# Dots of gathered expert rows in another instruction form, mask building moved behind the gathers, and two packing copies moved to ScalarE, in a two-block transformer kernel

## The reference

```python
q = (xc @ w_query).reshape(PEER_TOKEN_CHUNK, PEER_HEADS, 2, PEER_HALF)
s1 = jnp.einsum('thd,hnd->thn', q[:, :, 0], sub_keys_1)
s2 = jnp.einsum('thd,hnd->thn', q[:, :, 1], sub_keys_2)
v1, i1 = lax.top_k(s1, PEER_TOPK)
v2, i2 = lax.top_k(s2, PEER_TOPK)
cand = (v1[..., :, None] + v2[..., None, :]).reshape(...)
cand_idx = (i1[..., :, None] * PEER_NKEYS + i2[..., None, :]).reshape(...)
best, pos = lax.top_k(cand, PEER_TOPK)
idx = jnp.take_along_axis(cand_idx, pos, axis=-1)
g = jax.nn.softmax(best, axis=-1)
u = expert_u[idx]
act = jax.nn.gelu(jnp.einsum('td,thkd->thk', xc, u), approximate=False)
w = g * act
return jnp.einsum('thk,thkd->td', w, expert_v[idx])
```

## Time and profile before

| what | value |
|---|---|
| three runs | 1679.87, 1680.56 (median), 1681.11 us |
| the profiled execution, its own time | 1683.74 us |
| its span, first to last instruction | 1682.0 us |
| mean granted TensorE clock | 0.993 |
| busy: PE, DVE, ACT, POOL | 96%, 62%, 53%, 66% of the span |

### The profile page before, as it was taken

One profiled execution on the slowest core, in us unless ns is written; L12 is line 12 of the kernel. 1 busy time (PEld: TensorE's weight loads), 2 busy tenths in 40 slices (PEclk: granted clock), 3 DMA queues, 4 the chain that ended last, 5 costly groups with the idle time before them and its releaser, 6 DMA issues.

```text
span 1682.0 us, 29977 instructions
## 1 busy us (share of the span) xinstructions
PE 1619.4 (96%) x9740; PEld 1438.8 (86%) x9740; DVE 1041.9 (62%) x2176; ACT 895.5 (53%) x1631; POOL 1105.4 (66%) x604
## 2 busy tenths in 40 slices
PE   8989999999998898999999999999999999899998
PEld 7867899999888888999999897978888787788887
DVE  6274378996799987877888657653222367432223
ACT  5565555555444454555555557435545656554554
POOL 4815779999777776331332187448888895588886
PEclk9999999999999999999999999999999999999999
DMA  6633546665555557897888464125555564255553
GB/s 219 181 101 133 179 165 200 208 205 200 188 192 192 180 175 286 322 326 262 307 318 301 140 192 128 38 76 189 191 187 193 172 183 127 96 178 191 191 190 122
DMA packets 92531, 320.72 MB, mean 191 GB/s; under 512 B 10528, under 2 KB 10528, under 8 KB 92192
## 3 DMA queue, kind: packets, MB, share of 16 engines
q1 hardware_dynamic: 82272, 284.00, 50.9%
q0 software_dynamic: 9216, 33.56, 5.4%
q10 hardware_dynamic: 960, 2.13, 0.4%
HBM read 318.04 MB, written 1.05 MB: 190 GB/s over the span
## 4 chain that ended last, share of the span: by engine, by line
PE 84%; DVE 9%; issue 3%; ACT 2%; POOL 2%; DMA 0%; DVEq 0%; SPq 0%; POOLq 0%; ACTq 0%
PE col L980 10%; PE acc L682 7%; PE acc L683 7%; PE acc L684 7%; PE col L1335 7%; PE acc L1022 6%; PE col L984 5%; PE col L1339 4%; PE acc L1026 3%; PE col L1022 3%; PE mb L1022 3%; PE col L1026 2%; PE mb L1026 2%; PE col L719 1%; DVE expert_rows L2917 1%
## 5 line engine op out<-in xcount | busy, mean ns | idle before, releaser
L2146 POOL TENSOR_TENSOR w_lo<-w_raw,w_hi 128x1024 fp32r<-128x1024 f32 (+2 forms) x394 | 932.9, 2384 | 276.2 <-ACT w_hi L1551 248.9
L1551 ACT ACTIVATE w_hi<-w_raw 128x1024 fp32r<-128x1024 f32 (+1 forms) x539 | 565.6, 1052 | 281.0 <-PE mb L1026 120.3
L980 PE MATMUL col<-hT,w_hi 128*128 128x448 f32 x1024 | 235.2, 372 | 5.5 <-DVE acc L2707 5.4
L980 PEld LDWEIGHTS col<-hT,w_hi 128*128 128x128 f32 x1024 | 184.2, 190 | 19.5 <-DVE acc L2707 7.2
L2955 DVE TENSOR_TENSOR w_lo<-w_raw,w_hi 128x1024 fp32r<-128x1024 f32 x128 | 156.3, 1221 | 1.7 <-ACT w_hi L1551 1.6
L3242 DVE TENSOR_REDUCE mb<-col 128x256 f32<-128x512 f32 x64 | 44.8, 699 | 180.4 <-PE col L1339 180.4
L2318 POOL DMA_INDIRECT expert_rows<-in_expert_v,sparse_in x32 | 53.7, 1679 | 129.8 <-DVE W L2902 78.8
L984 PEld LDWEIGHTS col<-hT,w_lo 128*128 128x128 f32 x1024 | 134.7, 192 | 4.0
L984 PE MATMUL col<-hT,w_lo 128*128 128x224 f32 x1024 | 134.7, 274 | 0.0
L1022 PE MATMUL acc<-W,w_hi 128*128 128x448 f32 x512 | 127.7, 371 | 5.5 <-issue 5.5
L1335 PE MATMUL col<-hT,w_hi 128*128 128x512 f32 x512 | 128.8, 392 | 1.8 <-DVE hT L2450 1.8
(11 more groups left out here) (622 smaller groups left out, 3447.5 us busy)
## 6 DMA issues: line engine op xcount, KB each, us to landing
w_raw<-in_expert_u SPq DMA_DIRECT2D x128, 512.0 KB, 3.3
w_raw<-in_expert_v SPq DMA_DIRECT2D x128, 512.0 KB, 4.2
w_raw<-in_w_mlp SPq DMA_DIRECT2D x128, 512.0 KB, 3.3
w_raw<-in_w_in SPq DMA_DIRECT2D x24, 512.0 KB, 3.6
w_raw<-in_w_qkv_o SPq DMA_DIRECT2D x24, 512.0 KB, 4.1
w_raw<-in_w_query SPq DMA_DIRECT2D x16, 512.0 KB, 3.3
w_raw<-in_w_gate SPq DMA_DIRECT2D x16, 512.0 KB, 3.2
w_raw<-in_w_qkv_e SPq DMA_DIRECT2D x12, 512.0 KB, 3.7
```

The source lines that it names most:

```text
L980: mm(both, wh[:, k, :], hT[:, :, k, 0:DENSE], start=k == 0, stop=k == KD - 1, skip_group_check=True)
L1551: f(w_hi[:, s, 0:w], w_raw[:, s, 0:w], ACT.Copy).then_inc(sem(f"hi{s}"), 1)
L2146: g.tensor_tensor(w_lo[:, s, 0:w], w_raw[:, s, 0:w], w_hi[:, s, 0:w].bitcast(F32), ALU.subtract).then_inc(sem(f"lo{s}"), 1)
```

## The change

It has four edits, all in the PEER part.

- The two packing copies (weights and norm factor) leave VectorE. ScalarE makes them at gate step 2, directly ahead of the four transfers that need them, after a wait for the picks and for the norm factor; the transfers wait for a second semaphore, `weights_packed`.
- On VectorE one `both_halves` is called in the middle of the packing, between `gL` and `i1T`, one chunk earlier than it was; the loop that follows therefore makes one call fewer.
- The 32 dots use `scalar_tensor_tensor` with an accumulator output in place of `tensor_tensor_reduce`: (row x 1.0) x token, summed over the 1024 columns. The slots, buffers and steps stay.
- `block_masks` stands behind all gathers in `value_stage`.

```diff
--- before.py
+++ after.py
@@ -1731,7 +1731,17 @@
 
             def sparse_inputs():
 
+                top = slice(P - SPARSE, P)
+                act.wait_ge(sem("picks"), upto("picks", 1))
+                f(sparse_pack[top, :, SLOTS:2 * SLOTS],
+                  tk_bv[top, 1, :, :].rearrange("p h k -> p (h k)").rearrange(
+                      "p (g s) -> p g s", g=PARTS), ACT.Copy)
+                have_rstd(act, R_QUERY)
+                f(sparse_pack[top, :, 2 * SLOTS:PACK],
+                  rstd[top, 1:2].unsqueeze(1).to_broadcast([SPARSE, PARTS, 1]),
+                  ACT.Copy).then_inc(sem("weights_packed"), 1)
                 act.wait_ge(sem("packed"), 1)
+                act.wait_ge(sem("weights_packed"), 1)
                 for g in range(PARTS):
                     nc.scalar.dma_start(sparse_in[g * SPARSE:(g + 1) * SPARSE, :],
                                         sparse_pack[P - SPARSE:P, g, :]).then_inc(
@@ -2325,11 +2335,11 @@
                 used(pool, U0 + NKEYS - 1)
                 for i in range(EARLY, EARLY + 3):
                     expert_tile(i)
-                block_masks()
                 for i in range(EARLY + 3, SLOTS):
                     expert_tile(i)
                 for i in range(SLOTS, 2 * SLOTS):
                     expert_tile(i)
+                block_masks()
                 spatial_mask()
 
             norm_at = [FIRST[name] + 3 for name in ("qk", "query", "zba", "gate0", "q1", "gate1")]
@@ -2816,15 +2826,9 @@
             top = slice(P - SPARSE, P)
             key_of = [tk_sel[top, m, 1, :, :].rearrange("p h k -> p (h k)").rearrange(
                 "p (g s) -> p g s", g=PARTS) for m in range(2)]
-            then(v.scalar_tensor_tensor(out=sparse_pack[top, :, 0:SLOTS].bitcast(U32), in0=key_of[0],
-                                        scalar=float(NKEYS), in1=key_of[1], op0=ALU.mult,
-                                        op1=ALU.add))
-            then(v.tensor_copy(sparse_pack[top, :, SLOTS:2 * SLOTS],
-                               tk_bv[top, 1, :, :].rearrange("p h k -> p (h k)").rearrange(
-                                   "p (g s) -> p g s", g=PARTS)))
-            have_rstd(dve, R_QUERY)
-            then(v.tensor_copy(sparse_pack[top, :, 2 * SLOTS:PACK],
-                               over(rstd[top, 1:2], [SPARSE, PARTS, 1], 1)), "packed")
+            v.scalar_tensor_tensor(out=sparse_pack[top, :, 0:SLOTS].bitcast(U32), in0=key_of[0],
+                                   scalar=float(NKEYS), in1=key_of[1], op0=ALU.mult,
+                                   op1=ALU.add).then_inc(sem("packed"), 1)
             dve.wait_ge(sem("pk_T"), upto("pk_T", 1))
             def twice(m):
 
@@ -2833,6 +2837,7 @@
             then(v.tensor_scalar(gH[:, :, :], twice(mb[0][:, 0:SEQ]), GATE, None, ALU.mult))
             then(v.scalar_tensor_tensor(out=gL[:, :, :], in0=twice(mb[0][:, 0:SEQ]), scalar=GATE,
                                         in1=gH[:, :, :], op0=ALU.mult, op1=ALU.subtract))
+            both_halves()
             then(v.tensor_copy(i1T[:, :, :], twice(mb[0][:, SEQ:2 * SEQ])), "pk_E")
             dve.wait_ge(sem("pk_T"), upto("pk_T", 2))
             then(v.tensor_copy(i2T[:, :, :], twice(mb[1][:, 0:SEQ])), "pk_E")
@@ -2914,8 +2919,9 @@
                 dve.wait_ge(sem(f"tile_in{BUFFER_OF[i]}"), 16 * USE_OF[i])
                 if i == 0:
                     dve.wait_ge(sem("gained"), 1)
-                v.tensor_tensor_reduce(rows_[:, :], rows_[:, :], sparse_h[:, :], 1.0, 0.0, ALU.mult,
-                                       ALU.add, sparse_dot[:, i:i + 1]).then_inc(sem("tile_used"), 1)
+                v.scalar_tensor_tensor(out=rows_[:, :], in0=rows_[:, :], scalar=1.0, in1=sparse_h[:, :],
+                                       op0=ALU.mult, op1=ALU.mult,
+                                       accum_out=sparse_dot[:, i:i + 1]).then_inc(sem("tile_used"), 1)
 
             first_hot(0)
             second_hot(0)
```

## The result

The changed kernel takes 1668.63 us (median of four runs, 1668.53 to 1670.66), the kernel before 1680.84 (four runs, 1679.87 to 1681.15): a ratio of 0.9931, 95% interval 0.9914 to 0.9948, or 12.2 us less. A later measurement, beside new runs of the kernel before, gave 1668.89 against 1682.28, 0.9925 (0.9912 to 0.9939), or 13.4 us less. The forecast was 1666.6 us, 13.94 less, with a range of 1662 to 1674. The profiled execution has a span of 1666.8 us and a mean clock of 0.997 (before 1682.0 and 0.993).

What follows compares the result with a forecast made beforehand. TensorE was taken to bound the kernel, with two stalls to remove. Packing -6.45, masks -7.97 and dots +0.48 sum to -13.94 us, from 1680.56 to 1666.6 us; the 8-in-10 range is 1662 to 1674 us.

Steps and rivals of the forecast that it cites:

- What bounds it: TensorE, 84% of the chain; an edit counts only where TensorE stands still or another engine takes its place there.
- both stalls: TensorE waits at the packing and beside the first expert_v chunks, half clock behind each; removal gives -6.45 and -7.97 us.
- the moved stall: Rival: gathers in 632 to 645 us compete with weight transfers and stall TensorE again; about 1671 us, chance 0.11.
- The masks at nothing: The masks' 16.5 us behind the last gather cost nothing, as GpSimd waits 24.31 us for WST there.
- The dots at +0.48: The new form takes 1278 ns alone, 60 ns over the old; eight early dots add 0.48 us on the path.
- early dots still wait for GpSimd: Beside GpSimd's subtractions the eight early dots stay at about 3.0 us, so their 15.1 us of waits remain.
- The copies on ScalarE at nothing: Two copies at gate step 2, at most 0.7 us together, covered by ScalarE's 1.30 us wait for TensorE.
- The sum: -6.45 - 7.97 + 0.48 = -13.94 us, taken from 1680.56 us, gives 1666.6 us.
- The halved rate: Rival: the accumulator halves the dots' rate on VectorE, 1.34 us more per dot; 1686.6 us, chance 0.07.
- the form that does not wait: Rival: early dots in the new form escape GpSimd and nearly all of 15.1 us return; 1651 us, chance 0.06.
- lost edits: Rival: packing or masks gain nothing, a second cause standing right behind the first; 1673 to 1675 us, chance 0.03.
- the second rival: The new dot form does not wait for GpSimd, bringing back nearly all of 15.1 us; 1651 us, chance 0.06.

Runs made afterwards that it cites:

- e1: The kernel before, unchanged, run once more for its profile; 1687.77 us (one run).
- e2: The changed kernel with the mask building back between the third and fourth gather; 1675.61 us, 0.9972 of the kernel before.
- e4: The changed kernel with the dots as tensor_tensor_reduce again; 1670.21 us, 0.9931 of the kernel before.
- e6: The changed kernel with ScalarE's two packing copies one gate step earlier, at step 1; 1668.35 us, 0.9922 of the kernel before.
- e3: The changed kernel with both packing copies back on VectorE and the added both_halves taken out; 1675.64 us, 0.9964 of the kernel before.
- e9: The changed kernel with early gathers issued ahead of the step's subtraction, copies one gate step earlier, two more GpSimd waits; 1651.86 us, 0.9822 of the kernel before.
- e7: The changed kernel with only the two packing copies back on VectorE, the added both_halves kept; 1672.95 us (one run).

## Why the prediction was right, point by point

**What bounds it, and both stalls: right.** Each came out at its forecast size in the profile, -6.45 against -6.45 and -8.06 against -7.97, idle time and half clock together. That the second agrees to 0.1 us is no merit: forecast and difference were read from the same execution of the kernel before, and e1 and e2 have that stall smaller. Next late was nothing, as argued: the reductions wait for TensorE again, and 330 GB/s beside `expert_v` delay nobody (the moved stall did not occur). Undone one at a time, each stall cost 7.0 us against the changed kernel's median, and 5.4 against that of e4, which is as fast in every stretch and was measured beside them.

**The masks at nothing: right.** 8.68 us of the wait for `WST` are left over, and the norm has 16.67 more.

**The dots at +0.48: the step that was mis-sized.** I took 1278 ns from the row of the same form and size; it measured 1218, the lower bound that I had named, and the term is 0. That row takes its scalar from a tensor, one value per partition, adds where the dot multiplies, and writes to a tensor other than the rows; which of these makes the 60 ns was not tried. The rule that I weighed against it, of the Trainium skill (Vector Engine (DVE) Microarchitecture Reference, section Points that are easy to get wrong), would halve the rate. The measurement decides against it here: 1218 ns for 1024 columns, as long as the old form, and 82 ns for the read of the accumulator, which the old form has too. That early dots still wait for GpSimd was right (3014 ns).

**The copies on ScalarE at nothing: wrong by 0.80 us.** The failing step is "Ahead of that very row ScalarE waits 1.30 us for TensorE, and that covers it". I weighed only the copies, at most 0.7 us, against that cover. I named the four transfers behind them but did not ask when they could be issued: they had been issued beside the split, 2.5 us of issues that held nothing up, and the wait for the copies puts them behind it (e6).

**The sum.** In the terms that I had it is -6.45 - 8.06 + 0 + 0.80 = -13.7 us, against -13.94 forecast: two errors of the gates that nearly cancel (+0.48 forecast, +0.80 found). The measured medians say -12.2 and -13.4. That the forecast lies this near is in part that luck. What is left is the base: I took the stall beside `expert_v` from one execution, 3.2 us over the median, and subtracted it whole from the median. Three executions (two of the kernel before, one of e2) show that stall with 4.1 to 5.5 us of idle time, and mine was the longest of them; with e2's 5.9 us in place of 8.06 the sum is about -11.6. That is a likely reason why 1666.6 us was 2 us low, but not shown: the median executions left no trace, and the clock elsewhere moves them by as much.

**The rivals.** The halved rate and the form that does not wait are each excluded by one row (1218 and 3014 ns); a moved stall by the idle-free 120 us; lost edits by e2 and e3. But the 15.1 us that the second rival would have brought were real, and could be had by GpSimd's order in place of the form: 1651.86 us in e9, near the 1651 that the rival was priced at, though e9 also has the earlier copies and the shorter multiplication.

## What to carry to other kernels

A VectorE instruction that copies float32 from SBUF to SBUF, or takes two inputs from SBUF, waited here for the GpSimd subtraction that was running when it came due, at 32 x 4 as at 128 x 1024, and in both forms of the dot. One that reads PSUM did not (`gH`: 0.69 us at 418.36 beside a subtraction, and 0.69 with GpSimd idle). Look for rows of 2 to 3 us where the size says less than half of that, and then move GpSimd's own wait for that instruction ahead of its next long operation instead of changing the instruction. When work moves to an engine that also issues transfers, price the issues too: a semaphore that the engine sets itself just ahead of them kept them here from running beside its other work, and one step earlier was enough to avoid that. When a term is read from a stall, take it from more than one execution if there are more, or give it the width of the spread: the same stall came with 4.5 and 5.5 us in two executions of one kernel.

## What the runs showed of the hardware

- A wait of TensorE of 2.54 us left the clock at its full level (e7, next eight matmuls 1.89 us); the waits of 3.97 to 5.52 us in these two places were each followed by matmuls at the 1.2 GHz level. How long they stayed there differed behind the same wait: 3.36 us for eight matmuls behind 3.98 and 2.56 behind 3.99. The length of a single wait does not settle it: at 10.5 us the granted clock was 1.00 behind a wait of 3.01 us in the kernel before, and down to 0.50 behind one of 3.05 us at the same matmul in e7; at 1422 us of the changed kernel it was 0.50 behind a wait of 1.66 us, ahead of which TensorE had been busy for 1.05 of 2 us.
- The clock also falls in places that no edit touched, and not in every execution. With the table's three stretches taken out, the profiled executions spread from 1144.7 us (e2, and the changed kernel with 1144.8) to 1150.8 (e1). Runs of one kernel differ by 2 to 6 us; that the clock is most of it is likely, but the runs without a profile cannot show it.
- A `scalar_tensor_tensor` with an accumulator output shows as two instructions, the second a read of the accumulator of 0.08 us, and so does `tensor_tensor_reduce`. The Trainium skill (VectorE: DVE Perf Modes, section Two Vector instructions with no wait between them) counts it as two as well; it gives no duration.
